# The opening of a fused two-block kernel: silu(c) spread by a broadcast load, sine work behind the first subtractions, four shift tiles on TensorE

## The reference

```
cond = silu(c)                                            # 1024 values
mod  = (cond @ ada_w + ada_b).reshape(6, 1024)            # shift1, scale1, gate1, shift2, scale2, gate2
u    = rmsnorm(x, norm_mix) * (1 + scale1) + shift1
aq, ak, av, bq, bkv, biq, bik, biw, cq, ck, cv, g = split_cols(u @ w_in)
lam  = exp(sum(dl[0] * dl[1])) - exp(sum(dl[2] * dl[3])) + lam_init
bias = rel_bias[t5_bucket(dist)]                          # added to the attention logits
cos, sin = rotary_tables(positions_2)                     # first used in the second block
```

## Time and profile before

| | |
|---|---|
| median of 3 runs | 1026.4 us |
| profiled execution | 1031.09 us, span 1029.2 us |
| TensorE (PE) busy | 984.9 us, 96% |
| POOL busy | 729.1 us, 71% |
| DVE busy | 598.3 us, 58% |
| ACT busy | 490.2 us, 48% |

### The profile page before, as it was taken

The page is one execution under the profiler, slowest core; times in us unless marked ns, Lnnn a source line. Parts: engine busy times, 40 slices in busy tenths (PEclk is TensorE's granted clock), DMA queues, the critical chain, the costliest instruction groups (busy, mean ns, idle before and its releaser), DMA issues.

```text
span 1029.2 us, 21977 instructions
## 1 busy us (share of the span) xinstructions
PE 984.9 (96%) x7800; PEld 959.7 (93%) x7800; DVE 598.3 (58%) x1021; ACT 490.2 (48%) x804; POOL 729.1 (71%) x913
## 2 busy tenths in 40 slices
PE   7599899999899999999999999999999999999997
PEld 6588889999889999999899999999999999999996
DVE  5778996665886654121555557764254555676613
ACT  3265556654345554444344436444435444644441
POOL 5576675677667888767466668999656666799873
PEclk8799999999889999999899999999999999999999
DMA  9965556646443556555244444545523444445521
GB/s 354 376 234 198 204 179 225 220 150 246 164 164 127 201 190 238 180 190 196 80 173 149 145 156 167 202 163 185 188 80 126 162 163 163 155 173 187 184 100 42
DMA packets 28081, 184.70 MB, mean 179 GB/s; under 512 B 3011, under 2 KB 5488, under 8 KB 6128
## 3 DMA queue, kind: packets, MB, share of 16 engines
q1 hardware_dynamic: 25456, 167.22, 45.1%
q10 hardware_dynamic: 2560, 16.59, 4.5%
HBM read 182.73 MB, written 1.07 MB: 179 GB/s over the span
## 4 chain that ended last, share of the span: by engine, by line
PE 83%; DVE 8%; issue 4%; POOL 2%; ACT 2%; POOLq 0%; DVEq 0%; ACTq 0%
PE mm L539 24%; PE mm L540 24%; PE mm L541 24%; PE mm L571 2%; PE mm L557 1%; PE mm L558 1%; PE mm L559 1%; POOL w_lo L440 1%; DVE w_lo L1371 1%; ACT w_hi L973 1%; PE ps_s L871 1%; PE ps_o L886 1%; PE ps_o L922 1%; PE ps_s L660 1%; DVE merged L1682 1%
## 5 line engine op out<-in xcount | busy, mean ns | idle before, releaser
L440 POOL TENSOR_TENSOR w_lo<-raw,w_hi 128x256 fp32r<-128x256 f32 x876 | 702.0, 836 | 250.0 <-ACT w_hi L973 248.4
L539 PE MATMUL mm<-u_hi,w_hi 128*128 128x256 f32 x1608 | 466.5, 290 | 2.8 <-issue 2.6
L540 PE MATMUL mm<-u_lo,w_hi 128*128 128x256 f32 x1608 | 454.6, 283 | 0.0
L541 PE MATMUL mm<-u_hi,w_lo 128*128 128x256 f32 x1608 | 454.5, 283 | 0.0
L973 ACT ACTIVATE w_hi<-raw 128x1024 fp32r<-128x1024 f32 x291 | 306.9, 1055 | 170.2 <-PE mm L541 170.2
L539 PEld LDWEIGHTS mm<-u_hi,w_hi 128*128 128x128 f32 x1608 | 307.8, 191 | 9.2 <-issue 8.3
L540 PEld LDWEIGHTS mm<-u_lo,w_hi 128*128 128x128 f32 x1608 | 308.0, 192 | 2.1 <-issue 1.9
L541 PEld LDWEIGHTS mm<-u_hi,w_lo 128*128 128x128 f32 x1608 | 307.8, 191 | 0.0
L1371 DVE TENSOR_TENSOR w_lo<-raw,w_hi 128x1024 fp32r<-128x1024 f32 x72 | 93.8, 1302 | 127.4 <-ACT w_hi L973 125.7
L539 PE MATMUL mm<-mix_hi,w_hi 128*128 128x256 f32 x256 | 72.5, 283 | 0.1
L540 PE MATMUL mm<-h_lo,w_hi 128*128 128x256 f32 x256 | 72.4, 283 | 0.0
(11 more groups left out here) (284 smaller groups left out, 1332.0 us busy)
## 6 DMA issues: line engine op xcount, KB each, us to landing
raw<-weights SPq DMA_DIRECT2D x145, 1024.0 KB, 4.8
ada_raw<-ada ACTq DMA_DIRECT2D x14, 1024.0 KB, 4.9
ada_raw<-ada SPq DMA_DIRECT2D x6, 1024.0 KB, 10.8
ada_more<-ada SPq DMA_DIRECT2D x4, 1024.0 KB, 12.0
bias<-tab_scratch SPq DMA_DIRECT2D x1, 1536.0 KB, 13.4
dec<-decay ACTq DMA_DIRECT2D x1, 1536.0 KB, 7.8
x<-xT SPq DMA_DIRECT2D x1, 1024.0 KB, 9.2
out<-x SPq DMA_DIRECT2D x4, 256.0 KB, 2.2
```

The lines of the kernel that those rows point to most:

```text
L440: ins = nc.gpsimd.tensor_tensor(w_lo[:, s, at], r[:, at], hi[:, at], ALU.subtract)
L539: nc.tensor.matmul(dst, wh, rhs_hi(k), start=a, stop=False)
L540: nc.tensor.matmul(dst, wh, rhs_lo(k), start=False, stop=False)
L541: i = nc.tensor.matmul(dst, wl, rhs_hi(k), start=False, stop=b)
```

## The change

- A new first load on SP brings `c` to all 128 partitions as a row of 1024 (`c_b`). ACT takes tanh of it in two halves and DVE writes `(tanh + 1) * c`, twice the silu, to PSUM. The eight spreading matmuls go. POOL makes the copy of the row in SBUF (`cond_b`) by two steps of 128x1024 where DVE copied it. The factor 2 is taken out by factors of 0.5.
- Shift tiles 3, 7, 11 and 15 (chunks 1, 3, 5, 7) are loaded in the other layout and multiplied on TensorE (`ada_columns`: 8 matmuls with one column each). ACT adds the bias and puts the shift in place. Tile 3 stands before the spread of the inverse root; tiles 7, 11 and 15 stand inside `first_units`, ahead of chunks 2, 4 and 6.
- POOL's sine work is cut into ten steps, placed behind `low` of units 3, 5, 6, 8, 9, 10, 12, 13, 14 and 16. ACT's sine and cosine move to unit 18, POOL's steps on the cosine behind `low` of unit 22. The work for `lam` moves to units 3 (POOL), 9 and 12 (DVE) and 10 (ACT).
- The matmul for the bias table moves behind `first_units`, its copy and store on ACT behind unit 0. On SP the big load of the bias waits for that store, and the weight loads from unit 8 on stand behind it.
- The second pair of weights is loaded one place earlier; four small loads move from ACT's queue to SP's.
- `keep_warm` has 20 matmuls before the sums of squares (10 before), 20 behind the spread (7 before), and `CHUNK_WARM` behind the chunks (3 everywhere before).
- On DVE, adaptive steps 4 and 5 move behind the wait for the spread, and `first_lo` of a chunk comes one place earlier.

```diff
-PE_TILES = []
+PE_TILES = [3, 7, 11, 15]
+CHUNK_WARM = [0, 0, 0, 2, 3, 3, 3]
...
+TRIG_AT = [3, 5, 6, 8, 9, 10, 12, 13, 14, 16]
+SIN_AT = 18
...
+        sp.dma_start(c_b[:, :], bass.AP(c_row.tensor, 0, [[0, P], [1, D]])).then_inc(S["c_in"], 16)
         sp.dma_start(vec[:, :], cols).then_inc(S["small_in"], 16)
         sp.dma_start(ident[:, :], ident_d).then_inc(S["ident_in"], 16)
...
         ada_load(sp, 1)
         load(None, 0)
         ada_load(sp, 2)
+        load(None, 1)
         ada_load(sp, 3)
+        sp.dma_start(pos_i[:, :], bass.AP(positions.tensor, 0, [[0, P], [1, T]])).then_inc(S["pos_in"], 16)
+        sp.dma_start(relb_s[:, :], relb).then_inc(S["tab_in"], 16)
+        sp.dma_start(hot[:, :], onehot).then_inc(S["tab_in"], 16)
+        sp.dma_start(dlb[:, :], bass.AP(dl.tensor, 0, [[0, P], [1, 4 * HD]])).then_inc(S["dl_in"], 16)
         ada_load(sp, 4)
-        load(None, 1)
...
-        pool.wait_ge(S["dl_in"], 16)
-        for e in range(2):
-            G.tensor_tensor(dlp[:, e * HD:(e + 1) * HD], dlb[:, 2 * e * HD:(2 * e + 1) * HD],
-                            dlb[:, (2 * e + 1) * HD:(2 * e + 2) * HD], ALU.mult).then_inc(S["start_pool"], 1)
-
-        pool.wait_ge(S["small_in"], 16)
-        pool.wait_ge(S["pos_in"], 16)
-        own(G.tensor_copy(pos_f[:, :], pos_i[:, :]))
-        for e in range(2):
-            own(G.tensor_scalar(ang[:, e, :], pos_f[:, :], col("freq", e), None, ALU.mult))
+        pool.wait_ge(S["row_ready"], 2)
+        own(G.tensor_tensor(cond_b[:, :], cond_b[:, :], c_b[:, :], ALU.mult))
+        G.tensor_tensor(cond_b[:, :], cond_b[:, :], c_b[:, :], ALU.add).then_inc(S["cond_copied"], 1)
+
         big = 12582912.0
-        own(G.tensor_scalar(turns[:, :, :], ang[:, :, :], 1.0 / (2 * math.pi), big, ALU.mult, ALU.add))
-        own(G.tensor_scalar(turns[:, :, :], turns[:, :, :], big, None, ALU.subtract))
-        for cst in TWO_PI_PARTS:
-            own(G.tensor_scalar(part_turn[:, :, :], turns[:, :, :], cst, None, ALU.mult))
-            own(G.tensor_tensor(ang[:, :, :], ang[:, :, :], part_turn[:, :, :], ALU.subtract))
-        G.tensor_scalar(ang[:, :, :], ang[:, :, :], PI_BELOW, -PI_BELOW, ALU.min, ALU.max)\
-            .then_inc(S["start_pool"], 1)
+
+        def trig(n):
+
+            if n == 0:
+                pool.wait_ge(S["small_in"], 16)
+                pool.wait_ge(S["pos_in"], 16)
+                own(G.tensor_copy(pos_f[:, :], pos_i[:, :]))
+                own(G.tensor_scalar(ang[:, 0, :], pos_f[:, :], col("freq", 0), None, ALU.mult))
+            elif n == 1:
+                own(G.tensor_scalar(ang[:, 1, :], pos_f[:, :], col("freq", 1), None, ALU.mult))
+                own(G.tensor_scalar(turns[:, :, :], ang[:, :, :], 1.0 / (2 * math.pi), big, ALU.mult, ALU.add))
+            elif n == 2:
+                own(G.tensor_scalar(turns[:, :, :], turns[:, :, :], big, None, ALU.subtract))
+            elif n < 9:
+                if n % 2:
+                    own(G.tensor_scalar(part_turn[:, :, :], turns[:, :, :], TWO_PI_PARTS[n // 2 - 1], None, ALU.mult))
+                else:
+                    own(G.tensor_tensor(ang[:, :, :], ang[:, :, :], part_turn[:, :, :], ALU.subtract))
+            else:
+                G.tensor_scalar(ang[:, :, :], ang[:, :, :], PI_BELOW, -PI_BELOW, ALU.min, ALU.max)\
+                    .then_inc(S["start_pool"], 1)
 
         def lows(a, b):
 
@@ -487,14 +505,20 @@
...
-        for c in range(2):
+        for c in range(28):
             low(None, c)
-        pool.wait_ge(S["start_act"], 4)
-        own(G.tensor_tensor(cosT[:, :], cosT[:, :], cosT[:, :], ALU.mult))
-        own(G.tensor_scalar(cosT[:, :], cosT[:, :], -2.0, 1.0, ALU.mult, ALU.add))
-        for c in range(2, 12):
-            low(None, c)
-        lows(12, U_LAYER + SLOTS)
+            if c == 3:
+                pool.wait_ge(S["dl_in"], 16)
+                for e in range(2):
+                    G.tensor_tensor(dlp[:, e * HD:(e + 1) * HD], dlb[:, 2 * e * HD:(2 * e + 1) * HD],
+                                    dlb[:, (2 * e + 1) * HD:(2 * e + 2) * HD], ALU.mult).then_inc(S["start_pool"], 1)
+            if c in TRIG_AT:
+                trig(TRIG_AT.index(c))
+            if c == 22:
+                pool.wait_ge(S["start_act"], 3)
+                own(G.tensor_tensor(cosT[:, :], cosT[:, :], cosT[:, :], ALU.mult))
+                own(G.tensor_scalar(cosT[:, :], cosT[:, :], -2.0, 1.0, ALU.mult, ALU.add))
+        lows(28, U_LAYER + SLOTS)
...
-        pe.wait_ge(S["ident_in"], 16)
-        pe.wait_ge(S["cond_ready"], 1)
-        for k in range(KC):
-            c_ = cond[:, k:k + 1]
-            i = nc.tensor.matmul(ps_both[:, k * P:(k + 1) * P], bass.AP(c_.tensor, c_.offset, [c_.ap[0], [0, P]]), ident[:, :],
-                                 start=True, stop=True)
-        i.then_inc(S["spread_done"], 1)
-        pe.wait_ge(S["tab_in"], 2 * 16)
-        nc.tensor.matmul(ps_t[0:12, 0:3 * P], relb_s[:, :], hot[:, :], start=True, stop=True)\
-            .then_inc(S["tab_done"], 1)
...
-        keep_warm(WARM[4], 0)
+        pe.wait_ge(S["ident_in"], 16)
+        keep_warm(20, 0)
...
+        if PE_TILES:
+            pe.wait_ge(S["cond_ready"], 1)
+            ada_columns(PE_TILES[0])
         keep_warm(WARM[2], 0)
         spread(0)
-        keep_warm(WARM[2], 0)
+        keep_warm(20, 0)
...
+        def u_ready_ada(k, t):
+
+            a = 2 * (k + 1) + 1
+            if a in PE_TILES[1:]:
+                ada_columns(a)
+            pe.wait_ge(S["ulo_ready"], k + 1)
+
...
-                first_units(FIRST, c, c, u_ready(0), warm=3)
+                first_units(FIRST, c, c, u_ready_ada, warm=CHUNK_WARM)
+                if PE_TILES:
+                    pe.wait_ge(S["shift_taken"], len(PE_TILES))
+                pe.wait_ge(S["tab_in"], 2 * 16)
+                nc.tensor.matmul(ps_t[0:12, 0:3 * P], relb_s[:, :], hot[:, :], start=True, stop=True)\
+                    .then_inc(S["tab_done"], 1)
...
-        act.dma_start(pos_i[:, :], bass.AP(positions.tensor, 0, [[0, P], [1, T]])).then_inc(S["pos_in"], 16)
-        act.dma_start(relb_s[:, :], relb).then_inc(S["tab_in"], 16)
-        act.dma_start(hot[:, :], onehot).then_inc(S["tab_in"], 16)
-        act.dma_start(dlb[:, :], bass.AP(dl.tensor, 0, [[0, P], [1, 4 * HD]])).then_inc(S["dl_in"], 16)
+        act.wait_ge(S["c_in"], 16)
+        for half in range(2):
+            A(cond_b[:, 512 * half:512 * half + 512], c_b[:, 512 * half:512 * half + 512], ACT.Tanh, scale=0.5)\
+                .then_inc(S["th_half"], 1)
         act.wait_ge(S["small_in"], 16)
-        A(cond[:, :], vec[:, COLS["c"]:COLS["c"] + KC], ACT.Exp, scale=-1.0).then_inc(S["start_act"], 1)
...
-        act.wait_ge(S["tab_done"], 1)
-        A(tab_s[:, :], ps_t[0:12, 0:3 * P], ACT.Copy).then_inc(S["tab_evac"], 1)
-        act.wait_ge(S["tab_evac"], 1)
-        act.dma_start(tab_d, tab_s[:, :]).then_inc(S["tab_out"], 16)
         act.wait_ge(S["x_in"], 16)
         for half in range(2):
             A(x_sq[:, 4 * half:4 * half + 4, :], x[:, 4 * half:4 * half + 4, :], ACT.Square).then_inc(S["x_squared"], 1)
-        act.wait_ge(S["start_dve"], 1)
-        A(lam[:, 2:4], lam[:, 0:2], ACT.Exp).then_inc(S["start_act"], 1)
...
-            if k == 1:
-                act.wait_ge(S["start_pool"], 3)
-                A(sinT[:, :], ang[:, 1, :], ACT.Sin).then_inc(S["start_act"], 1)
-                A(cosT[:, :], ang[:, 0, :], ACT.Sin, scale=0.5).then_inc(S["start_act"], 1)
             if k == 2:
                 high(None, 2)
...
+            if c == 0:
+                act.wait_ge(S["tab_done"], 1)
+                A(tab_s[:, :], ps_t[0:12, 0:3 * P], ACT.Copy).then_inc(S["tab_evac"], 1)
+                act.wait_ge(S["tab_evac"], 1)
+                act.dma_start(tab_d, tab_s[:, :]).then_inc(S["tab_out"], 16)
+            if c == 10:
+                act.wait_ge(S["start_dve"], 1)
+                A(lam[:, 2:4], lam[:, 0:2], ACT.Exp).then_inc(S["start_act"], 1)
+            if c == SIN_AT:
+                act.wait_ge(S["start_pool"], 3)
+                A(sinT[:, :], ang[:, 1, :], ACT.Sin).then_inc(S["start_act"], 1)
+                A(cosT[:, :], ang[:, 0, :], ACT.Sin, scale=0.5).then_inc(S["start_act"], 1)
...
-        dve.wait_ge(S["start_act"], 1)
-        own(V.tensor_scalar(cond[:, :], cond[:, :], 1.0, None, ALU.add))
-        own(V.reciprocal(cond[:, :], cond[:, :]))
-        V.tensor_tensor(cond[:, :], cond[:, :], vec[:, COLS["c"]:COLS["c"] + KC], ALU.mult).then_inc(S["cond_ready"], 1)
+        for half in range(2):
+            at = slice(512 * half, 512 * half + 512)
+            dve.wait_ge(S["th_half"], half + 1)
+            V.scalar_tensor_tensor(ps_s[half][:, :], cond_b[:, at], 1.0, c_b[:, at], ALU.add, ALU.mult)\
+                .then_inc(S["row_ready"], 1)
+        dve.wait_ge(S["cond_th"], 1)
+        V.scalar_tensor_tensor(cond[:, :], cond[:, :], 1.0, vec[:, COLS["c"]:COLS["c"] + KC], ALU.add, ALU.mult)\
```

(40 more changed lines are left out.)

33 lines of the change are left out of this document (18 added, 15 removed).

## The result

The changed kernel takes 1033.37 us (median of 8 runs, 1030.03 to 1037.26); the kernel before, run on the same chip beside it, takes 1026.18 (8 runs). The ratio is 1.0060, 95% interval [1.0040, 1.0081]: slower by some 7 us. Run once more on another chip it gave 1033.75 us and 1.0055 [1.0034, 1.0076]. The forecast was 1029.0 with a range of 1022.8 to 1032.5 and 0.47 for slower: the sign was right, the size too small by 4.4 us (2.6 of 7.2), and the time lies 0.9 us above the upper end of the range. The profiled execution is the slowest of the 8, 1037.26 us, with a span of 1035.3.

What follows compares the result with a forecast made beforehand. The prediction took TensorE, busy 96% of the span, as the bound, with its 10.6 us opening wait as the aim. +3.6 + 1.0 - 0.7 - 1.3 = +2.6 on 1026.4 gave 1029.0 us, range 1022.8 to 1032.5.

Steps and rivals of the forecast that it cites:

- Step 1: Opening up to the spread: first `t_u` moves by +1.2 to 24.5 us, with ends of -0.8 and +2.0.
- Step 2: First `t_u` to TensorE's start: 11.1 us, so TensorE starts at 35.6 us, 0.8 earlier than before.
- faster rival: Opening: spread at 22.5, TensorE starts at 32.2, clock stays high, tile 7 done at 36.4; 1022.8 us, chance 24%.
- Step 3: Loop through TensorE: DVE stands before chunk 3 for shift tile 7; unit 3 starts at 56.3 us, +3.6.
- Step 4: POOL's sine work between subtractions: before unit 6 about 1.6 us of pieces against 0.6 of room, +1.0.
- Step 5: Later units: DVE's lag at its first logits absorbs 0.7 us, ACT's exp table load happens earlier, -1.3.
- bias rival: Big bias load holds unit 8's weights until near 73 us, ACT stands at its `w_hi`; 1033 us, chance 7%.

Runs made afterwards that it cites:

- one-block run: The changed kernel with the `lam` products and all ten sine steps in one block between `low` of units 2 and 3, tiles kept: 1029.94 us, ratio 1.0023.
- the kernel before with its order mended: The kernel before with `low` of unit 2 ahead of POOL's sine work and ACT's sine and cosine behind the first units: 1023.95 us, ratio 0.9973.
- the three fixes together: The changed kernel without shift tiles on TensorE, sine work in one block behind `low` of unit 3, its `w_hi` behind chunk 3's `u_hi`: 1021.42 us.

## Why the prediction was right or wrong

**Step 1, first `t_u` at 24.5: 22.73 measured** (22.75 in the second profile), inside its ends. The clock rose during the 20 `keep_warm` (6.24 us for 40 passes, not 8.4), and the tile cost 3.1 us, not 2.0, since the clock was low while it ran. The 14 passes behind it took 3.33 us, as before; without tiles they took 1.81, a cost of the tile that the step did not have.

**Step 2, 11.1 us from there to the start: 9.4.** The two `u_lo` took 0.48 and did not collide; I had named that as worth 1.4. TensorE started at 32.2, and so one of my own signs of being wrong ("TensorE starts before 33 us") was met, yet the sign held, since the next step does not depend on the start alone. The faster rival had this start, 32.2, but with 1 to 2 us of idle time before it: the 20 `keep_warm` ran in 4.80 us and left 4.9, and the 18 matmuls behind ran at 0.21 us each.

**Step 3, +3.6 at unit 3: +6.0 and +6.1.** The mechanism was right: ACT's wait for tile 7, DVE's stand before chunk 3, unit 3 released by POOL. The size failed in two places. First, I counted tile 7 only and took tiles 11 and 15 to be hidden. DVE waited for them too, 2.11 and 3.23 us, as TensorE's chunks went at half the clock (1.07 and 1.12 in the second profile, where the clock had risen by then). Second, I let the clock rise for good after the start. It fell again in one profile and did not rise before 44 us in the other, and the faster rival's condition ("as its idle time is then only 1 to 2 us the clock stays high") named the wrong cause: TensorE was busy in 40 to 50 us and the clock was 0.50. With one matmul a tile, or tile 7 early, it was 1.00. In 40 to 42 us it was 0.50 to 0.60 in all five profiles with the whole of tile 7 behind chunk 1, and 1.00 in all five in which it is shortened, done earlier or left to DVE.

**Step 4, +1.0 at unit 6: +2.4 in the first profile, +0.8 in the second,** at unit 5. The step counted what stands before unit 6 and passed over what stands before unit 5: the products for `lam` and the first sine step, 4.0 us between `low` of units 3 and 5 (58.6 to 62.6). The products took 2.56 us where they had taken 0.60 before, beside DVE's adaptive steps. Unit 5 waited 2.09 us in the first profile, so a second sign of being wrong (a unit from 5 to 10 that waits over 2 us) was met there, and 0.20 in the second.

**Step 5, -2.0: +4.9 between units 12 and 16, +1.8 in all from unit 5 to the end. This is the step that failed in sign.** The table load did go from unit 13, and DVE's lag did not absorb anything. POOL's sine steps on units 8 to 16 (I had written "from unit 8 on there is room of over 4 us") filled that room (POOL is busy 29.43 of 30 us in 80 to 110, below, and DVE 28.57) and made DVE late; `low` of units 17 and 18 stood beside the first head's softmax, whose four steps took 0.78, 0.62, 0.84 and 0.70 us instead of 0.35, 0.28, 0.48 and 0.70, and TensorE waited 3.5 for them. Without the reduction, and with the sine in one block, the stretch is back at 15.1 us. In the same 30 us by the clock the one-block run has POOL busy for 20.30 us and DVE for 26.12. The two rows, the changed kernel's first (columns as in the stretches above):

```profile
80.00:110.00 30.00, 30.00 (x226) 27.36 (x225) 28.57 (x60) 16.54 (x33) 29.43 (x32) 1.00 0.59 211
```

```profile
80.00:110.00 30.00, 29.05 (x223) 26.74 (x223) 26.12 (x68) 15.64 (x31) 20.30 (x24) 1.00 0.54 207
```

In the one-block run the same steps are just as slow (0.79, 0.64, 0.85), so the collision alone is not it: DVE's late arrival is the larger part: from its read of the key-value sums (L1582) to the first logits it needs 28.3 us there (97.28 - 68.97) and 31.5 in the changed kernel (104.88 - 73.35). Over all thirteen profiles it is 31.4 to 32.6 us where the sine steps are spread and 28.3 to 29.5 where they are not. The clock adds the rest: behind TensorE's wait of 3.5 us it was 0.50 (116 to 118 us), and it took 5.0 us to the copy of unit 16 (119.36 - 114.39), where the one-block run, with a wait of 0.95 and the clock at 1.00, took 3.5 (110.91 - 107.45).

The Trainium skill (SBUF — State Buffer, Who interferes with whom) has GpSimd and VectorE share one port pair by an exclusive lock, which the first to come holds for its whole instruction. The trace agrees, in that many of DVE's small index-score and softmax steps took about twice as long beside POOL (0.78 against 0.35 us, 1.85 against 1.00 for a pair of index-score steps).

**The bias rival** had its mechanism right and its size wrong: ACT waited 5.0 us for unit 8's weights (2.0 in the second profile), but the load took 7.2 us, not 13.4, and TensorE was held elsewhere. Moving it gave 1.4 us between the medians by itself and 1.9 once the rest was mended, neither of them shown.

**Luck.** The 2.8 us won behind `m_lo` were in no term of the prediction; without them the time would have been further off. They also make up much of what the versions without tiles gain over before: in the version without tiles `m_lo` comes 1.9 us later than in the second profile of before, and the span is still 2.7 shorter.

**What stays open:** why those 2.8 us are won (the kernel before with its order mended needs 755.4 us there, the variants of the changed one 751.7 to 754.3), and what exactly makes the clock fall. Where they are won can be read. Behind the MLP's matmuls DVE writes one tile of `x` for each 96 passes of TensorE. Timeline of DVE, the second profile of before and that of the changed kernel:

```profile
417.35 0.48 DVE L1746 SCALAR_TENSOR_TENSOR x<-mm,mod,x 128x256 f32<-128x256 f32 x1 [5.83 <-PE mm L541]
428.87 0.48 DVE L1746 SCALAR_TENSOR_TENSOR x<-mm,mod,x 128x256 f32<-128x256 f32 x1 [5.57 <-PE mm L541]
```

```profile
417.28 0.48 DVE L1779 SCALAR_TENSOR_TENSOR x<-mm,mod,x 128x256 f32<-128x256 f32 x1 [5.87 <-PE mm L565]
428.54 0.48 DVE L1779 SCALAR_TENSOR_TENSOR x<-mm,mod,x 128x256 f32<-128x256 f32 x1 [5.64 <-PE mm L565]
```

That is 11.52 us a round against 11.26, or 0.120 us a pass against 0.117, both at the full clock. It is 11.52 in all three profiles of the kernel before and its reordered version, and 11.26 in all ten of the changed kernel and its variants; eight such rounds give 2 us. No run here tells what sets the pace.

## What to carry to other kernels

Work moved to the bounding engine is not priced by its own length: it stands in that engine's program order, and whoever feeds that engine waits until its turn comes; put such work where the engine waits anyway. Room on a helper engine, counted unit by unit, is used up once by everything moved there: follow it to the next point where two helpers meet, here POOL's subtractions and DVE's softmax. When one change removes a wait and adds something else, price the two apart: the removal here was worth some 2 us, and the shift tiles alone cost 9 to 10.

## What the runs showed of the hardware

- Matmuls with one column did not keep the clock up, though TensorE was busy with hardly a gap (0.6 us at most). In all seven profiles with 48 such passes the granted clock had been 1.00 and was 0.50 in 18 to 20 us. Of the six profiles with the 32 of the sums alone, four fell to 0.50 as well (both of before, its reordered version, and the three fixes together) and two stayed at 1.00 up to 24 us. So the clock fell in seven of seven profiles with 48 passes and in four of six with 32, and no more than that is shown.
- A small operation can be held for the length of the other engine's. Timelines of DVE and POOL, changed kernel:

```profile
6.94 2.36 POOL L458 TENSOR_TENSOR cond_b<-cond_b,c_b 128x1024 f32<-128x1024 f32 x1 [6.01 <-DVE ps_s L1411]
7.04 2.29 DVE L1419 TENSOR_SCALAR gain<-vec 128x8 f32<-128x8 f32 x1
9.37 0.17 DVE L1417 SCALAR_TENSOR_TENSOR a_pre<-vec 128x8 f32<-128x8 f32 x1
```

  A step on 128x8 elements took 2.29 us beside a product of POOL, and its neighbour 0.17.
- POOL's `low` for one unit took 2.8 to 4.8 us in the changed kernel, with different work of DVE beside it. A sine step kept its 1.50 us beside adaptive steps that read one operand from PSUM, and took 2.35 and 2.34 us (at 77.09 and 86.81 us, without tiles) beside DVE steps with both operands in SBUF.
- A wait of TensorE of 3.5 us in mid-kernel was followed by some 4 us at half the clock and cost 1.5 us; waits of 0.8 to 1.7 us at the same place were followed by none.
